# Products of constants in six pauses of TensorE, in a two-block transformer kernel

## The chip, the core and the metric

One Trainium2 chip, of which the kernel uses one core. The metric is the device time of one execution in microseconds (us), the median of several runs. Five engines work side by side, each through its own queue in order: TensorE (PE, matrix products), VectorE (DVE), ScalarE (ACT), GpSimd (POOL) and SyncE (SP, which issues transfers here). They wait for each other through semaphores. TensorE's clock has two levels, 1.2 and 2.4 GHz; the profile shows which of them was granted, as a share of the higher (0.50 or 1.00, or a mean between them).

## The reference

256 tokens of width 1024, with 16 learned tokens in front, go through two blocks, all in float32:

```python
# first block: two layers
for layer in range(2):
    h = rms_norm(hs, norm_mix_pre[layer])
    mix = pool_mixer(h, ...) if layer == 0 else sliding_window_attention(h, k_blk, v_blk, ...)
    hs = hs + rms_norm(mix, norm_mix_post[layer])
    h = rms_norm(hs, norm_ffn_pre[layer])
    hs = hs + rms_norm(swiglu(h, w_gate_up[layer], w_down[layer]), norm_ffn_post[layer])
    # after layer 0: keys and values from rms_norm(hs, kv_norm)
# second block: one layer, on the last 256 tokens
z = rms_norm_2(h, norm1_g) @ w_in            # three mixers: stick-breaking attention, mLSTM, spatial gating
h = h + concatenate([ya, yb, yc]) @ w_out
h = h + hierarchical_moe(rms_norm_2(h, norm2_g), ...)   # 32 experts, two per token
gate = sigmoid(rms_norm_2(h, ple_norm_g) @ ple_gate_w)
out = rms_norm_2(h + gate * (p @ ple_proj_w), final_g)
```

## The kernel before

Activations lie with the channels on the 128 partitions, in eight chunks of 256 or 272 tokens. Every large weight is split into a high and a low part of float32r, and so is every activation; a product is then three products of parts (`mm3`, L1268: high x high, low x high, high x low). SyncE streams the weights into `ring` (three slots), ScalarE writes the high part of each piece (L710), VectorE the low part (L720), into buffers `wh`/`wl` and `third_h`/`third_l`; each piece that is done adds one to the semaphore `lo_done`. The experts' weights go into `wring` and are used whole.

TensorE's queue runs through the stages in the order in which they are written. Between two stages lies a seam: the result must be squared, summed over the channels by a product with ones (`sum_squares`, L1259, into bank 6), turned into a factor on ScalarE (L691, L692), applied and added to the residual on VectorE and GpSimd (L1779, L564), and split into high and low parts again. TensorE has little or nothing to do meanwhile. The seams here:

- *queries* (L1306): behind the first feed-forward block. The high parts of x come one chunk at a time (`xh_ready`, ScalarE L871); for each, eight products. Then the sums, the low parts (L1312), keys and values.
- *the second feed-forward block* (`ffn_pe` with l = 1, L1199): the same pattern, x from ScalarE L805, two pieces of weights, eight products per chunk; then sums and L1207 with the low parts, then the long loop of L1268.
- *norm1*: eight sums of squares, each waiting for a square of ScalarE, then the products with `w_in` (`z`, L1268), which wait for both parts of x (`x_ready`, VectorE L1794).
- *norm2*: eight sums, then the router's products (L1592, 36 columns), 16 transposes (L1598) whose results ScalarE and VectorE split into `h2h` and `h2l`, and 32 products of the projection (L1609), whose banks ScalarE empties one after the other.
- *before the gathers*: four bfloat16 products of zeros open banks 0 to 3 (L1712), once `h2h`, `h2l` are complete; then the gathers of tokens for the first experts (L1623, L1624), which wait for VectorE's selection (`psel_ready`).
- *the last gate*: behind the sixteenth round of experts, whose results are combined in L1674, VectorE adds the experts' output to the residual and forms the low parts (L2343); the products with `w_ple` (L1268) follow, and behind the first 24 of them the eight sums of the norm.

`cst` is a table of constants in SBUF (identity, masks and the like), loaded at the start. Of the eight PSUM banks, 7 holds nothing that is still needed at the seams where the change writes it, and bank 0 nothing before L1712.

Of the kernel before, what the change touches and what calls it, by code (L numbers as in the profile page):

```python
# [7 lines left out]
BF16 = mybir.dt.bfloat16  # L8
# [6 lines left out]
P = 128  # L15
# [3 lines left out]
SEQ = 256  # L19
# [121 lines left out]
def bass_two_blocks(nc, a, out):  # L141
# [4 lines left out]
    with ctx:  # L146
# [5 lines left out]
        def sem(name):  # L152
            if name not in sems:
                sems[name] = ctx.enter_context(nc.semaphore(name))
            return sems[name]
# [24 lines left out]
        cst = sb("cst", [P, NC])  # L180
# [990 lines left out]
        def onehot(i):  # L1171

            return small[:, 200 + i * NB * NE:200 + (i + 1) * NB * NE].rearrange("p (b e) -> p b e", b=NB)

        def ffn_pe(pe, mm3, sum_squares, l, n):

            gu, dn, pre, post = f"w_gu{l}", f"w_dn{l}", f"ffnpre{l}", f"ffnpost{l}"
            xa, xb = (xhT, xlT) if l == 0 else (xh, xl)
            base = FIRST_PIECE[gu]

            def piece(i, j):
                f = i * 2 + j
                pe.wait_ge(sem("lo_done"), f + (base + 1))
                pe.wait_ge(sem("up_ready"), f + (l * NF - 1))
                w = split_buffer(gu, i, j)
                for k in range(KD):
                    for g in range(2):
                        at = slice(k * 256 + g * P, k * 256 + g * P + P)
                        ins = mm3(ps[:, 2 * j + g, 0:n], [x[:, at] for x in w], (xa[:, k, 0:n], xb[:, k, 0:n]),
                                  k == 0, k == KD - 1)  # L1190
                ins.then_inc(sem("gu_psum"), 1)

            def with_high(k):

                pe.wait_ge(sem("xh_ready"), 2 * l * KD + k + 1)
                for j in range(2):
                    for part, w in enumerate(split_buffer(gu, 0, j)):
                        for g in range(2):
                            pe.matmul(ps[:, 2 * j + g, 0:n], w[:, k * 256 + g * P:k * 256 + g * P + P], xa[:, k, 0:n],  # L1199
                                      start=(k == 0 and part == 0), stop=False)  # L1200

            def with_low(j):
                w = split_buffer(gu, 0, j)[0]
                for k in range(KD):
                    pe.wait_ge(sem("x_ready"), 2 * l * KD + k + 1)
                    for g in range(2):
                        ins = pe.matmul(ps[:, 2 * j + g, 0:n], w[:, k * 256 + g * P:k * 256 + g * P + P], xb[:, k, 0:n],  # L1207
                                        start=False, stop=(k == KD - 1))
                ins.then_inc(sem("gu_psum"), 1)

            pe.wait_ge(sem("lo_done"), base + 2)
            for k in range(KD):
                with_high(k)
            for c in range(KD):
                sum_squares(pre, c, n)
            with_low(0)
            with_low(1)
            piece(1, 0)
            piece(1, 1)
            with pe.Fori(2, NF // 2) as i:  # L1220
                for j in range(2):
                    piece(i, j)
            base = FIRST_PIECE[dn]
            for c in range(KD):
                if c >= 2:
                    pe.wait_ge(sem("sq_ready"), SQ0[post] + c - 1)
                for j in range(2):
                    pe.wait_ge(sem("lo_done"), base + 2 * c + j + 1)
                    w = split_buffer(dn, c, j)
                    for k in range(NF // 2):  # L1230
                        at = slice(k * P, (k + 1) * P)
                        f = j * (NF // 2) + k
                        if c == 0:
                            pe.wait_ge(sem("act_split"), l * NF + f + 1)
                        ins = mm3(ps[:, 4 + c % 2, 0:n], [x[:, at] for x in w],
                                  (acth[:, f, 0:n], actl[:, f, 0:n]), f == 0, f == NF - 1)
                    ins.then_inc(sem("dn_psum"), 1)
                if c:
                    sum_squares(post, c - 1, n)
            sum_squares(post, KD - 1, n)  # L1240
# [3 lines left out]
        def _(pe):  # L1244
# [54 lines left out]
                return [x[:, at] for x in split_buffer("w_q", c // 4, c // 2 % 2)]  # L1299

            pe.wait_ge(sem("lo_done"), FIRST_PIECE["w_q"] + 2)
            for k in range(KD):
                pe.wait_ge(sem("xh_ready"), KD + k + 1)
                for c in range(4):
                    for part, w in enumerate(q_weights(c, k)):
                        mm(ps[:, c, 0:SEQ], w, xh[:, k, 0:SEQ], start=(k == 0 and part == 0), stop=False)  # L1306
# [117 lines left out]
            ffn_pe(pe, mm3, sum_squares, 1, SEQ)  # L1424


            for c in range(KD):
                sum_squares("norm1", c, SEQ)
            def sgu_mix():

                pe.wait_ge(sem("sgu_v"), 1)
                pe.wait_ge(sem("sgw_masked"), 1)
                for g in range(SG):
                    ins = mm(ps[:, 7, g * P:(g + 1) * P].rearrange("p (b c) -> p b c", b=NB), sgw[:, g, :],
                             vc[:, :, g * SG_D:(g + 1) * SG_D], start=True, stop=True)
                ins.then_inc(sem("sgu_psum"), 1)
# [149 lines left out]

            for c in range(KD):
                sum_squares("norm2", c, SEQ)
            for b in range(NB):
                for k in range(KD):  # L1590
                    pe.wait_ge(sem("xn_ready"), KD + k + 1)
                    ins = mm(ps[:, 0, b * 36:(b + 1) * 36], mix[:, k, b * P:(b + 1) * P], rw[:, k, :],  # L1592
                             start=(k == 0), stop=(k == KD - 1))
# [86 lines left out]
            def extra(b):  # L1680
# [24 lines left out]
                with pe.Else():  # L1705
                    pe.sem_inc(sem("over_pe"), len(OVER["pe"]) * (ROUNDS - 1))

            pe.wait_ge(sem("h2h_ready"), 4)
            pe.wait_ge(sem("h2l_ready"), 4)
            pe.wait_ge(sem("diag_ready"), 1)  # L1710
# [44 lines left out]
            combine((yh, yl), places[(TEAMS - 1) % 2][:, :], True)  # L1755


            for c in range(KD):
                piece = FIRST_PIECE["w_ple"] + c // 2
                pe.wait_ge(sem("lo_done"), piece + 1)  # L1760
                if c >= 4:
                    pe.wait_ge(sem("ple_scaled"), c - 3)
                for k in range(KD):
                    pe.wait_ge(sem("x_ready"), 4 * KD + k + 1)
                    at = slice(k * 256 + c % 2 * P, k * 256 + c % 2 * P + P)
                    ins = mm3(ps[:, c % 4, 0:SEQ], [x[:, at] for x in split_buffer("w_ple", c // 4, c // 2 % 2)],
                              (xh[:, k, 0:SEQ], xl[:, k, 0:SEQ]), k == 0, k == KD - 1)
                ins.then_inc(sem("ple_psum"), 1)
                if c == 0:
                    for q in range(KD):  # L1770
                        sum_squares("ple", q, SEQ)
# [737 lines left out]
```

## Time and profile before

| | us |
|---|---|
| three timed runs | 1070.78, 1072.61, 1072.77 (median 1072.61) |
| the profiled execution | 1068.52 |
| its span, first to last instruction | 1066.8 |
| TensorE busy in it | 974.7 (91%) |
| VectorE, ScalarE, GpSimd busy | 540.2, 416.1, 155.6 |
| mean granted clock of TensorE | 0.954 |

The span leaves out some 1.7 us of start and end. Times inside the profile are counted from the span's start. The chain of waits that ended last is TensorE for 85% of the span. A matmul's busy time includes its way through the array, so products in a row overlap: what one costs is the distance between starts, or the length of a run divided by its count.

### The profile page before, as it was taken

The page shows a single profiled execution, that of the slowest core. Times are in us where ns is not written, and L with a number is a line of the kernel's source. Part 1 is how long each engine was busy: PE and PEld are TensorE (multiplying, and loading weights), DVE is VectorE, ACT ScalarE, POOL GpSimd, SP SyncE. Part 2 cuts the span into 40 slices and gives each one's busy share as a digit, 9 for nine tenths or more (in the row PEclk, how much of TensorE's full clock was granted, in tenths as well). Part 3 has the DMA queues.
Part 4 walks back from the last instruction along what each step waited for, and adds up shares of the span by engine and source line. Part 5 has one row for each costly group of instructions (what it writes and reads, how often), then busy time and mean ns, then how long its engine had stood idle before and what let it go on. Part 6 is the DMA issues. An engine that isn't in the chain of part 4 may idle for free.

```text
span 1066.8 us, 16807 instructions
## 1 busy us (share of the span) xinstructions
PE 974.7 (91%) x6776; PEld 819.1 (77%) x6777; DVE 540.2 (51%) x986; ACT 416.1 (39%) x697; POOL 155.6 (15%) x216
## 2 busy tenths in 40 slices
PE   3799999998989999999969999879699999999876
PEld 2599999998869899999959999578454555545365
DVE  5655454438783655554463548574523333433254
ACT  4543333347575534434454556633211111111153
POOL 5432323011001433331120000000100000000000
PEclk8899999999989999999998999788899999999988
DMA  7435453568522254534543412049079999999601
GB/s 290 157 106 202 167 172 134 189 185 205 141 80 89 93 213 158 188 131 163 214 164 127 159 52 82 1 168 396 3 283 417 420 420 420 419 420 419 260 1 40
DMA packets 36797, 211.99 MB, mean 199 GB/s; under 512 B 2528, under 2 KB 16112, under 8 KB 17520
## 3 DMA queue, kind: packets, MB, share of 16 engines
q1 hardware_dynamic: 36720, 210.91, 52.4%
q8 instruction: 55, 0.90, 0.3%
q14 instruction: 22, 0.18, 0.1%
HBM read 209.83 MB, written 1.07 MB: 198 GB/s over the span
## 4 chain that ended last, share of the span: by engine, by line
PE 85%; DVE 7%; ACT 3%; issue 2%; POOL 2%; DMA 0%; POOLq 0%; DVEq 0%; ACTq 0%
PE ps L1268 49%; PE ps L1651 11%; PE ps L1665 5%; PE ps L1259 3%; PE ps L1674 3%; PE ps L1623 2%; PE ps L1199 2%; DVE wl L720 2%; PE ps L1624 1%; DVE mix L1779 1%; PE ps L1306 1%; PE ps L1372 1%; PE ps L1207 1%; PE ps L1609 1%; PE ps L1592 1%
## 5 line engine op out<-in xcount | busy, mean ns | idle before, releaser
L720 DVE TENSOR_TENSOR wl<-ring,wh 128x2048 fp32r<-128x2048 f32 (+3 forms) x106 | 210.3, 1987 | 193.9 <-ACT wh L710 193.9
L710 ACT ACTIVATE wh<-ring 128x2048 fp32r<-128x2048 f32 (+3 forms) x106 | 176.1, 1665 | 267.2 <-PE ps L1268 265.2
L1268 PE MATMUL ps<-xh,wh 128*128 128x256 f32 (+3 forms) x632 | 180.5, 286 | 6.4 <-DVE xl L2343 6.4
L1268 PE MATMUL ps<-xh,wl 128*128 128x256 f32 (+3 forms) x632 | 179.0, 283 | 0.0
L1268 PE MATMUL ps<-xl,wh 128*128 128x256 f32 (+3 forms) x632 | 178.8, 283 | 0.0
L1268 PEld LDWEIGHTS ps<-xh,wh 128*128 128x128 f32 (+3 forms) x632 | 117.6, 186 | 7.8 <-issue 7.5
L1268 PEld LDWEIGHTS ps<-xh,wl 128*128 128x128 f32 (+3 forms) x632 | 117.6, 186 | 0.1
L1268 PEld LDWEIGHTS ps<-xl,wh 128*128 128x128 f32 (+3 forms) x632 | 117.5, 186 | 0.0
L1268 PE MATMUL ps<-acth,wh 128*128 128x272 f32 (+1 forms) x352 | 101.1, 287 | 0.0
L1268 PE MATMUL ps<-actl,wh 128*128 128x272 f32 (+1 forms) x352 | 100.0, 284 | 0.0
L1268 PE MATMUL ps<-acth,wl 128*128 128x272 f32 (+1 forms) x352 | 100.0, 284 | 0.0
L1268 PE MATMUL ps<-xhT,wl 128*128 128x272 f32 x320 | 92.6, 289 | 0.0
L1268 PE MATMUL ps<-xlT,wh 128*128 128x272 f32 x320 | 92.2, 288 | 0.0
L1268 PE MATMUL ps<-xhT,wh 128*128 128x272 f32 x320 | 91.3, 285 | 0.0
L575 POOL TENSOR_TENSOR sq<-sq 128x256 f32<-128x256 f32 (+1 forms) x15 | 19.1, 1274 | 436.0 <-ACT sq L685 436.0
L2327 DVE TENSOR_TENSOR yl<-ps,yh 128x512 fp32r<-128x512 f32 x32 | 20.6, 686 | 91.3 <-ACT yh L1137 91.3
L1268 PEld LDWEIGHTS ps<-acth,wh 128*128 128x128 f32 x352 | 66.5, 189 | 0.2
L1268 PEld LDWEIGHTS ps<-acth,wl 128*128 128x128 f32 x352 | 66.1, 188 | 0.2
L1268 PEld LDWEIGHTS ps<-actl,wh 128*128 128x128 f32 x352 | 66.2, 188 | 0.0
L1651 PE MATMUL ps<-wring,xb_even 128*64 128x512 f32 x256 | 60.0, 607 | 4.1 <-issue 4.0
L1268 PEld LDWEIGHTS ps<-xhT,wh 128*128 128x128 f32 x320 | 60.4, 189 | 0.0
L1268 PEld LDWEIGHTS ps<-xlT,wh 128*128 128x128 f32 x320 | 60.1, 188 | 0.0
(402 smaller groups left out, 1859.5 us busy)
## 6 DMA issues: line engine op xcount, KB each, us to landing
wring<-in_w_eg SPq DMA_DIRECT2D x32, 2048.0 KB, 14.3
ring<-in_w_gu SPq DMA_DIRECT2D x22, 2048.0 KB, 8.2
wring<-in_w_ed SPq DMA_DIRECT2D x16, 2048.0 KB, 12.9
ring<-in_w_dn SPq DMA_DIRECT2D x16, 1408.0 KB, 6.1
ring<-in_w_z SPq DMA_DIRECT2D x7, 2048.0 KB, 7.7
ring<-in_w_out SPq DMA_DIRECT2D x4, 1152.0 KB, 5.2
ring<-in_w_q SPq DMA_DIRECT2D x8, 512.0 KB, 6.2
ring<-in_w_o SPq DMA_DIRECT2D x8, 512.0 KB, 16.0
```

Source lines behind the costliest of these rows:

```text
L575: pool.tensor_tensor(even, even, odd, ALU.add).then_inc(sem("sq_paired"), 1)
L710: ins = act.activation(to, src, ACT.Copy)
L720: ins = dve.tensor_tensor(to, src, h.bitcast(F32), ALU.subtract)
L1199: pe.matmul(ps[:, 2 * j + g, 0:n], w[:, k * 256 + g * P:k * 256 + g * P + P], xa[:, k, 0:n], start=(k == 0 and part == 0), stop=False)
L1207: ins = pe.matmul(ps[:, 2 * j + g, 0:n], w[:, k * 256 + g * P:k * 256 + g * P + P], xb[:, k, 0:n], start=False, stop=(k == KD - 1))
L1259: mm(ps[:, 6, 0:n], ones[0:rows, :], square_at(name, c + 1 - chunks)[0:rows, 0:n], start=(c < chunks), stop=(c == last))\
L1268: ins = mm(o, p, q, start=first and n == 0, stop=last and n == 2)
L1623: mm(out, h2h[:, k, at], select[:, k, :], start=(k == 0), stop=False)
L1651: ins = mm(ps[rows, 4, :], x[:, k, rows], chunk(b, c)[:, j, i * 512:(i + 1) * 512], start=(k == 0), stop=(k == KD - 1))
L1665: ins = mm(ps[rows, 6 + i, :], heT[:, k, rows], chunk(b, GU_CHUNKS)[:, j, k * D + i * 512:k * D + (i + 1) * 512], start=(k == 0), stop=(k ...
L1674: ins = mm(ps[:, c // 2, c % 2 * SEQ:(c % 2 + 1) * SEQ], y[:, c * P:(c + 1) * P], weights, start=False, stop=last and y is parts[-1], skip ...
L2327: dve.tensor_tensor(yl[:, i * 512:(i + 1) * 512], ps[:, 6 + i, :], yh[:, i * 512:(i + 1) * 512].bitcast(F32), ALU.subtract).then_inc(sem(" ...
```

## The change

A new function, `stay_busy`, issues n products of 128 columns of constants (as bfloat16) with 512 columns of constants, each into the same bank with start and stop set, and without semaphore. It is called at seven places in TensorE's queue, at six seams: 8 at the queries, 8 in the second feed-forward block, 17 ahead of and 15 behind the sums of norm1, 4 behind the sums of norm2, 11 ahead of L1712, 24 ahead of the last gate; 87 in all. No other line changes.

```diff
+        def stay_busy(pe, bank, n):
+            weights, moving = cst[:, 0:P // 2].bitcast(BF16), cst[:, 0:SEQ].bitcast(BF16)
+            for _ in range(n):
+                pe.matmul(ps[:, bank, :], weights, moving, start=True, stop=True)
...
             pe.wait_ge(sem("lo_done"), base + 2)
+            if l:
+                stay_busy(pe, 7, 8)
             for k in range(KD):
                 with_high(k)
...
             pe.wait_ge(sem("lo_done"), FIRST_PIECE["w_q"] + 2)
+            stay_busy(pe, 7, 8)
...
             ffn_pe(pe, mm3, sum_squares, 1, SEQ)
+            stay_busy(pe, 7, 17)
             for c in range(KD):
                 sum_squares("norm1", c, SEQ)
+            stay_busy(pe, 7, 15)
...
                 sum_squares("norm2", c, SEQ)
+            stay_busy(pe, 7, 4)
...
+            stay_busy(pe, 0, 11)
             pe.wait_ge(sem("h2h_ready"), 4)
...
             combine((yh, yl), places[(TEAMS - 1) % 2][:, :], True)
+            stay_busy(pe, 7, 24)
             for c in range(KD):
                 piece = FIRST_PIECE["w_ple"] + c // 2
```

In the rows below, `ps` is PSUM, `cst` the constants, and what stands in brackets are the semaphores for which a product waits. Lines of the changed kernel are some 6 to 13 higher. TensorE at the queries' seam, before:

```order
L1268 MATMUL ps<-actl,wh 128x272
L1259 MATMUL ps<-sq,ones 128x272 [waits sq_ready] x2
L1306 MATMUL ps<-xh,third_h 128x256 [waits xh_ready,lo_done]
L1306 MATMUL ps<-xh,third_l 128x256
L1306 MATMUL ps<-xh,third_h 128x256
L1306 MATMUL ps<-xh,third_l 128x256
```

and now:

```order
L1276 MATMUL ps<-actl,wh 128x272
L1267 MATMUL ps<-sq,ones 128x272 [waits sq_ready] x2
L1179 MATMUL ps<-cst 128x512 [waits lo_done]
L1179 MATMUL ps<-cst 128x512 x7
L1315 MATMUL ps<-xh,third_h 128x256 [waits xh_ready]
L1315 MATMUL ps<-xh,third_l 128x256
L1315 MATMUL ps<-xh,third_h 128x256
```

Eight products of constants stand between the last sum of the block before and the first product with x; the first of them has taken over the wait for the split weights. TensorE at norm1, before:

```order
L1268 MATMUL ps<-actl,wh 128x256
L1259 MATMUL ps<-sq,ones 128x256 [waits sq_ready] x2
L1259 MATMUL ps<-sq,ones 128x256 [waits sq_ready,r_ready]
L1259 MATMUL ps<-sq,ones 128x256 [waits sq_ready] x7
L1268 MATMUL ps<-third_h,xh 128x256 [waits x_ready,lo_done]
L1268 MATMUL ps<-third_l,xh 128x256
L1268 MATMUL ps<-third_h,xl 128x256
```

and now:

```order
L1276 MATMUL ps<-actl,wh 128x256
L1267 MATMUL ps<-sq,ones 128x256 [waits sq_ready] x2
L1179 MATMUL ps<-cst 128x512 x17
L1267 MATMUL ps<-sq,ones 128x256 [waits sq_ready,r_ready]
L1267 MATMUL ps<-sq,ones 128x256 [waits sq_ready] x7
L1179 MATMUL ps<-cst 128x512 x15
L1276 MATMUL ps<-third_h,xh 128x256 [waits x_ready,lo_done]
L1276 MATMUL ps<-third_l,xh 128x256
L1276 MATMUL ps<-third_h,xl 128x256
```

The sums keep their waits, and a batch stands on either side of them. TensorE ahead of the gathers, before:

```order
L1615 MATMUL ps<-small,cst 128x32
L1616 MATMUL ps<-small,ones 128x32
L1617 MATMUL ps<-small,ones 128x32
L1712 MATMUL ps<-work 128x512 [waits diag_ready,h2l_ready,h2h_ready]
L1712 MATMUL ps<-work 128x512 x3
L1623 MATMUL ps<-psel,h2h 128x256 [waits psel_ready]
```

and now:

```order
L1627 MATMUL ps<-small,cst 128x32
L1628 MATMUL ps<-small,ones 128x32
L1629 MATMUL ps<-small,ones 128x32
L1179 MATMUL ps<-cst 128x512 x11
L1725 MATMUL ps<-work 128x512 [waits diag_ready,h2l_ready,h2h_ready]
L1725 MATMUL ps<-work 128x512 x3
L1635 MATMUL ps<-psel,h2h 128x256 [waits psel_ready]
```

The 11 follow the last small products of the routing directly and wait for nothing; the waits of the products that open the banks come behind them.

## Rows read from the trace of the kernel before

**Rows 1.** The page: TensorE's granted clock in 40 equal slices, in tenths.

```profile
PEclk8899999999989999999998999788899999999988
```

**Rows 2.** Stretches: length, busy PE, PEld, DVE, ACT, POOL, clock, DMA share, GB/s.

```profile
249.42:252.00 2.58, 0.00 (x0) 0.03 (x1) 1.63 (x4) 1.48 (x4) 0.20 (x1) 1.00 1.06 356
...
252.10:255.40 3.30, 3.30 (x16) 3.30 (x17) 3.23 (x7) 2.48 (x8) 1.71 (x3) 0.50 1.11 368
...
347.90:350.40 2.50, 0.00 (x0) 0.01 (x1) 1.57 (x4) 1.43 (x4) 0.19 (x1) 1.00 0.96 406
...
544.40:549.20 4.80, 0.00 (x0) 0.00 (x0) 3.83 (x8) 4.77 (x6) 1.76 (x2) 0.98 0.02 5
...
555.56:559.20 3.64, 0.00 (x1) 0.00 (x0) 3.64 (x8) 3.02 (x8) 0.00 (x0) 1.00 0.49 131
...
560.20:566.00 5.80, 5.80 (x27) 5.80 (x28) 4.40 (x8) 3.36 (x3) 0.00 (x0) 0.50 0.49 209
...
736.80:746.90 10.10, 10.10 (x44) 9.83 (x45) 5.20 (x24) 2.48 (x5) 0.00 (x0) 0.50 0.98 406
...
757.30:763.90 6.60, 4.79 (x18) 3.70 (x20) 5.27 (x22) 0.60 (x1) 2.72 (x5) 0.50 0.01 1
...
1023.05:1026.70 3.65, 3.65 (x17) 3.65 (x18) 3.11 (x7) 1.71 (x5) 1.05 (x1) 0.50 0.02 4
```

**Rows 3.** Chain that ended last: start us, length us, engine and line.

```profile
252.00 9.35 PE ps L1306 x64
...
350.42 9.42 PE ps L1199 x64
...
550.35 0.83 DVE hs L564
...
553.78 2.73 DVE wl L720
...
742.07 3.46 PE ps L1598 x16
...
745.53 7.71 PE ps L1609 x32
...
1031.52 19.95 PE ps L1268 x168
```

**Rows 4.** TensorE in order of time, router and gathers: start, length, idle before.

```profile
735.15 3.72 PE L1592 MATMUL ps<-rw,mix 128*128 128x36 f32 x17 [1.44 <-DVE mix L1779]
...
757.67 0.63 PE L1712 MATMUL ps<-work 128*128 128x512 bf16 x1 [3.41 <-issue]
...
757.67 1.49 PE L1712 MATMUL ps<-work 128*128 128x512 bf16 x3 [3.41 <-issue]
...
760.60 0.58 PE L1623 MATMUL ps<-psel,h2h 128*128 128x256 f32 x1 [1.44 <-DVE psel L1936]
```

**Rows 5.** ScalarE and GpSimd in order of time, three seams.

```profile
252.79 0.51 ACT L871 ACTIVATE xh<-hs,vec 128x256 fp32r<-128x256 f32 x1 [0.61 <-POOL hs L564]
...
351.15 0.51 ACT L805 ACTIVATE xh<-hs,vec 128x256 fp32r<-128x256 f32 x1 [0.56 <-POOL hs L564]
...
551.66 2.70 POOL L564 TENSOR_TENSOR hs<-hs,mix 128x256 f32<-128x256 f32 x1 [0.76 <-DVE mix L1779]
```

**Rows 6.** The last gate in order of time: TensorE, VectorE, ScalarE.

```profile
1023.05 0.55 PE L1268 MATMUL ps<-xh,wh 128*128 128x256 f32 x1 [6.42 <-DVE xl L2343]
...
1027.69 1.03 PE L1259 MATMUL ps<-sq,ones 128*128 128x256 f32 x4
...
1022.43 3.73 DVE L2343 SCALAR_TENSOR_TENSOR xl<-hs,vec,xh 128x256 fp32r<-128x256 f32 x8
...
1028.32 1.33 ACT L685 ACTIVATE sq<-hs 128x256 f32<-128x256 f32 x4 [3.56 <-PE ps L1259]
```

**Rows 7.** Stretches that the change doesn't touch, columns as in rows 2.

```profile
303.30:310.00 6.70, 6.70 (x39) 5.08 (x38) 6.56 (x27) 3.36 (x13) 0.00 (x0) 0.50 0.25 51
...
774.20:777.60 3.40, 3.40 (x10) 1.43 (x11) 0.00 (x0) 0.00 (x0) 0.00 (x0) 0.52 0.00 0
```

## What the change should do to the time

> **What bounds the kernel now.** I read the page first: TensorE is busy for 91% of the span and makes up 85% of the chain that ended last, and in ten of the 40 slices its granted clock is below nine tenths [rows 1]. So TensorE sets the time, and part of its work is done at the lower of its two clock levels (1.2 GHz, granted 0.50) instead of the higher (2.4 GHz, granted 1.00). Then I read stretches at the seams between stages [rows 2]: each time the engine has nothing to do (busy 0.00) and the row behind it, where it works again, has clock 0.50. At 249.42 it stops for 2.58 us, and the next 3.30 us of work run at 0.50; from 555.56 it does nothing for 3.64 us, and the 5.80 us of work from 560.20 run at 0.50. The rows that end in a bracket [rows 4, 6] give three more such pauses, 1.44, 3.41 and 6.42 us, with 0.50 behind them at 736.80, 757.30 and 1023.05 [rows 2]. Behind the 2.50 us at 347.90 the same loop as at 252.00 is as long as there, 9.42 against 9.35 us [rows 3]. The chain of waits [rows 3] shows that the work behind the pauses is itself on the path to the end, in long unbroken pieces of TensorE.
>
> What a product costs at either level: 168 split products of 256 columns took 19.95 us at 1.00, so 0.119 us each [rows 3]; 17 of them fill 3.65 us at 0.50, so 0.214 us each [rows 2]. A stretch of low clock of length t in which the engine works without waiting costs 1 - 0.119/0.214 = 0.44 t.
>
> **The change part by part.** Nothing is removed or moved. 87 products of 512 columns are added (8, 8, 17, 15, 4, 11, 24), none with a semaphore of its own, all into a bank that its next user starts anew. The nearest row for such a product is L1712, bfloat16, 512 columns, at 0.50: three in 1.49 us, of which one alone is 0.63, so (1.49 - 0.63)/2 = 0.43 us each [rows 4]. At 1.00 I take half, 0.22 us (by the ratio of the 256-column products it would be 0.24). So the batches last 1.8, 1.8, 3.7, 3.3, 0.9, 2.4 and 5.3 us if the clock holds. What hides them are the pauses: 2.58, 2.50, 4.80, 4.6 (555.56 to 560.20), 1.44, 3.4 and 6.4 us [rows 2, 4, 6]. Each is shorter than its pause, so the batches themselves cost nothing; if the clock were low throughout, the first two would last 3.4 us and overrun by 0.9 us each. Two of them now take over the wait for the split weights (lo_done), which was met before the pause began.
>
> *The queries' seam* (8 products, then L1306, 64 products from 252.00, 9.35 us [rows 3]). At 1.00 throughout, eight products per chunk of x need 0.95 us. The second chunk comes only at 252.79 + 0.51 = 253.30 [rows 5]; with the 0.14 us from there to TensorE and 7 x 0.95 the loop ends at 260.1 and not at 261.35. Gain 1.25 us; bounds 0 and 0.44 x 3.4 = 1.5. The sums, L1312 and ScalarE's next split (it waits for L1312) follow TensorE, so it is passed on.
>
> *The second feed-forward block* (8, then L1199, 64 products in 9.42 us from 350.42 [rows 3]). Likewise: second chunk at 351.66 [rows 5], end at 351.80 + 6.65 = 358.45 and not 359.84. Gain 1.4 us; bounds 0 and 1.5. L1207 then waits for nothing: x's low parts and the pair sums are done by about 360.
>
> *norm1* (17 ahead of the eight sums, 15 behind). The sums are set by VectorE and GpSimd, not by TensorE: the last add of the stream, on GpSimd, takes 2.70 us from 551.66, and normalising can't start before a split on VectorE ends at 553.78 + 2.73 = 556.51 [rows 3, 5]. So the 17 gain nothing. The 15 stand ahead of L1268, whose first 5.8 us run at 0.50 [rows 2]: worth 0.44 x 5.8 = 2.6 us. Off this goes a new hole: the last add but one ends at 550.35 + 0.83 = 551.18 [rows 3]; with its square and its sum, some 0.4 us each, TensorE is then through at about 552.1, and does nothing until the last add is done at 554.36, about as long as at 249.42, where the clock fell. If it falls here, some 8 of the 15 run at 0.43, as long as the low stretch at 252.10, and 7 at 0.22: 5.0 us, from the end of the last sum at 555.56 until 560.5 instead of 560.20. I take 2.3 us; bounds 0.8 (all 15 at 0.43, 1.8 us over) and 2.6.
>
> *norm2* (4). The clock falls into the router's products (L1592) and stays at 0.50 for 10.10 us although the engine is counted busy all that time [rows 2], with 36-column products and then transposes [rows 3, 4]. Four products move that fall later, they don't stop it. At best everything to 746.9 runs high: the last 16 of L1592 and the 16 transposes, 0.216 us each [rows 3], save 0.094 each or 3.0 us, and the first 1.4 us of L1609 0.7, together 3.7 us; at worst 0. I take 0.7, near the low end, for 0.9 us of work against 10 us of low clock. It is passed on: ScalarE empties L1609's banks one by one and VectorE's routing waits for that.
>
> *Before the gathers* (11). The four products of L1712 aren't on the path: the first gather waits for the selection made by VectorE until 760.60 [rows 4]. After them TensorE has some 2 us of nothing again, so I expect the 16 gather products still mostly at 0.50. Bounds 0 and 16 x 0.094 = 1.5; I take 0.3.
>
> *The last gate* (24, ahead of L1268 at 1023.05, after 6.42 us idle [rows 6]). Its first products run at 0.50 [rows 2] and the sums behind the first 24 start at 1027.69. With the clock high they keep pace with x's low parts, eight in 3.73 us from 1022.43, so until 1026.16 + 0.14 + 3 x 0.119 = 1026.7. Gain 1.0 us, passed on since ScalarE's last four squares wait for those sums [rows 6]; bounds 0 and 1.7.
>
> Sum: 1.25 + 1.4 + 2.3 + 0.7 + 0.3 + 1.0 = 7.0 us. Against the profiled execution, 1068.52 us with a span of 1066.8, that is 1061.5; the three timed runs lie 2 to 4 us above it, at a median of 1072.61, and the forecast goes by that: **1065.6 us**.
>
> The rule of the Trainium skill that weighs here is in "TensorE: Matmul & The Clock Gate", Part 4 (PE-mode transpose): the high clock doesn't engage for transposes. The trace agrees as far as it goes, with 0.50 through all 16 of L1598 [rows 2, 3]. By it alone norm2's batch would gain nothing and the sum would be 6.3.
>
> **The rivals.** *Everything holds.* norm2 and the gathers reach their upper bounds: 3.0 + 1.2 us more, 1061.4. Against it speaks that both have a thin stretch right behind the batch.
>
> *The clock falls elsewhere.* The idle time before a fall isn't one number: below 2.6 us at 249.42, above 4.6 at 544.40 (0.98 over 4.80 us) [rows 2]. So where a fall comes depends on something beside the work, and low stretches that the change doesn't touch, 6.70 us at 303.30 and 3.40 at 774.20 [rows 7], can come out longer after the shift. One more low stretch like that at 774.20 (0.44 x 3.4 = 1.5 us), the two seams with the shortest pauses falling in only half of the runs even before (half of 1.25 + 1.4, 1.3 us), and nothing from norm2 (0.7) take 3.5 us off the gain: 1069.1. The same page says (Part 1, What's actually happening) that the gate's window runs free of the kernel, so the switch falls differently from run to run; these rows agree, and by it no single run gives the sum above.
>
> *The products don't count.* No row shows bfloat16 products of constants raising the clock; the four of L1712 came and went at 0.50. If the gate ignores them, every fall comes where it did, the batches of the first seams are over by then, and only the 24 lose something: by 1020 about 15 are done, 9 more at 0.43 end at 1023.9, 0.8 us late. 1073.4, no change.
>
> *Slower: the batches run at the low level.* If the clock is down when the 15 and the 24 start and they don't bring it back, they take 6.45 and 10.3 us, 1.8 and 3.9 us past their pauses, with L1268 behind them still at 0.50: 1078.3. It decides from the point where a batch at 0.43 is longer than its pause. Against it: the clock came back under ordinary work each time.
>
> **How the numbers follow.** Forecast 0.50, everything holds 0.13, falls elsewhere 0.20, don't count 0.10, slower 0.07. A measurement of this kernel tells 0.2% (2.1 us) from no change. Faster by more: 0.50 + 0.13 + 0.17 of the third = 0.80; within: the rest of the third and the fourth, 0.13; slower 0.07. The range runs from 1061 (the upper case) to 1071 (beyond the third case), leaving out most of the last two.
>
> **What would show it.** Right: granted clock 1.00 in L1306, in L1199 and in the first z products; L1306 some 8.1 us long, L1199 8.0 us; L1268 behind norm1 starting within 0.4 us of 4.7 us after the last sum; mean clock above 0.954. Wrong in size: the fall merely moved into the sums or the gathers. Wrong altogether: L1306's first products still 0.214 us apart behind eight constant products, or a first product of a stage that waits for a batch and not for x.

## The result, and the profile after

The changed kernel took **1057.61 us** (median of 8 runs, 1055.99 to 1065.58), the kernel before, beside it, 1070.26 us (8 runs, 1065.18 to 1072.77): a ratio of 0.9888, 95% interval 0.9865 to 0.9911. So it is faster by 12.0 us, with 9.5 to 14.4 in the interval. The forecast had the direction right and the size wrong: 7.0 us of gain, 1065.6 us, and a range whose lower end was 1061. The profiled execution lasted 1058.62 us. The ratios here and below leave out runs over 1.5% above the fastest of their kernel: one of six of the kernel with only the 15 behind norm1's sums, and five of twelve of that with 143 narrow products.

The page after, its span and granted clock:

```profile
span 1056.9 us, 16974 instructions
...
PEclk8799999999999999999999999789799999999998
```

Beside [rows 1] the eights of slices 12, 22, 28 and 39 are gone (slice 12 is the stretch around 303 us, where nothing was added; slice 22 holds z's start, slice 28 the router), and six slices are below nine tenths, where there were ten. The mean granted clock is 0.967 instead of 0.954.

TensorE after, in order of time, at norm1 and at the last gate (start, length, what, idle before and releaser):

```profile
543.75 3.62 PE L1179 MATMUL ps<-cst 128*128 128x512 bf16 x16
548.62 3.26 PE L1267 MATMUL ps<-sq,ones 128*128 128x256 f32 x14 [1.25 <-ACT sq L685]
554.21 0.70 PE L1267 MATMUL ps<-sq,ones 128*128 128x256 f32 x2 [2.33 <-ACT sq L685]
554.74 3.40 PE L1179 MATMUL ps<-cst 128*128 128x512 bf16 x15
559.55 0.36 PE L1276 MATMUL ps<-third_h,xh 128*128 128x256 f32 x1 [1.41 <-DVE xl L1808]
...
1006.54 5.13 PE L1179 MATMUL ps<-cst 128*128 128x512 bf16 x23
1014.33 0.36 PE L1276 MATMUL ps<-xh,wh 128*128 128x256 f32 x1 [2.67 <-DVE xl L2357]
```

One record each of the 17 and of the 24 is missing from the trace. Fifteen of the products take 3.40 us, 0.23 each, where the forecast for the high clock was 0.22. Behind the 15 and behind the 24 the stage's first product waits for VectorE's xl, not for the batch. Stretches after (columns as in rows 2):

```profile
253.96:262.33 8.37, 8.14 (x65) 7.93 (x66) 8.27 (x17) 7.14 (x16) 3.75 (x4) 1.00 1.08 284
...
559.55:566.00 6.45, 6.45 (x54) 6.45 (x55) 4.41 (x8) 3.82 (x4) 0.16 (x2) 1.00 0.46 198
...
736.90:740.30 3.40, 3.40 (x19) 3.40 (x19) 2.79 (x15) 1.79 (x3) 0.00 (x0) 0.51 1.02 424
740.42:747.20 6.78, 6.78 (x33) 5.96 (x32) 2.63 (x13) 3.38 (x9) 0.00 (x0) 1.00 0.47 195
...
754.03:764.27 10.24, 8.58 (x34) 7.74 (x35) 4.37 (x14) 1.20 (x2) 2.69 (x4) 0.50 0.00 1
...
1014.40:1017.80 3.40, 3.13 (x23) 2.93 (x24) 3.05 (x7) 1.64 (x5) 1.06 (x1) 1.00 0.00 0
```

At the queries, at z (norm1) and at the last gate the clock is 1.00, where [rows 2] had 0.50. At the router only 3.4 us are left of the 10.1 at 0.50. Around the gathers it is worse than before: 10.24 us at 0.50, the four products of L1734 behind them included, and before 6.6.

Where the two executions drift apart, by the starts of the same products (before, after, and the distance of after from before):

| product | before | after | distance |
|---|---|---|---|
| first of the queries (L1306, now L1315) | 252.00 | 253.96 | +1.96 |
| first of z (L1268, now L1276) | 560.20 | 559.55 | -0.65 |
| gating products amid the z stage (L1434, L1445) | 598.00 | 594.71 | -3.29 |
| router (L1592, L1604) | 735.15 | 732.05 | -3.10 |
| first gather (L1623, L1635) | 760.60 | 754.74 | -5.86 |
| first expert product (L1651, L1663) | 771.33 | 767.72 | -3.61 |
| first down product (L1665, L1677) | 785.78 | 779.39 | -6.39 |
| last team but one, combining (L1674, L1686) | 990.62 | 982.65 | -7.97 |
| last combining | 1013.05 | 1004.32 | -8.73 |
| first sum of the last gate (L1259, L1267) | 1027.69 | 1017.97 | -9.72 |

The execution starts with a loss of 2 us that no added product explains (none has run by then): the clock was low for 6.7 us in the first feed-forward block. From there to the first expert product the changed kernel gains 5.6 us, and 1.0 at the last gate, together 6.6; of this some 0.5 us lies between the queries and the second feed-forward block, where nothing was added. But 5.1 us come from another place where nothing was added, between the first expert product and the last combining. What changed there shows in TensorE's order of time, first team of experts, before:

```profile
771.33 1.04 PE L1651 MATMUL ps<-wring,xb_even 128*64 128x512 f32 x2 [2.23 <-issue]
774.12 4.43 PE L1651 MATMUL ps<-wring,xb_even 128*64 128x512 f32 x11 [1.75 <-issue]
```

and after:

```profile
767.72 4.87 PE L1663 MATMUL ps<-wring,xb_even 128*64 128x512 f32 x13 [2.20 <-issue]
```

Before, the engine stopped for 1.75 us after two of the products, with nothing to wait for ("issue"), and the clock was low behind that hole [rows 7, second row]. From the first expert product to the first down product it took 14.45 us before, and 11.67 after. The experts' waits as a whole, 764 to 1012 us (waited for: us in total, times, longest), before:

```profile
PE ps L1651 <- issue: 5.2, 4, 2.2
```

and after:

```profile
PE ps L1663 <- issue: 2.2, 1, 2.2
```

### The profile page after: what moved, and what is told of

It is laid out like the page before. It is cut to its first block, busy times and chain, and to the rows that moved or that the text cites. A ratio compares the mean times of both kernels' runs of the same rounds, so it can differ in the third digit from the quotient of the medians.

```text
span 1056.9 us, 16974 instructions
## 1 busy us (share of the span) xinstructions
PE 982.0 (93%) x6858; PEld 813.5 (77%) x6864; DVE 540.0 (51%) x986; ACT 416.2 (39%) x697; POOL 155.7 (15%) x216
## 4 chain that ended last, share of the span: by engine, by line
PE 85%; DVE 8%; ACT 3%; POOL 2%; issue 2%; DMA 0%; POOLq 0%; DVEq 0%; ACTq 0%
PE ps L1276 49%; PE ps L1663 11%; PE ps L1677 5%; PE ps L1267 3%; PE ps L1686 3%; PE ps L1635 2%; PE ps L1205 2%; PE ps L1636 2%; DVE wl L720 2%; DVE mix L1793 1%; PE ps L1213 1%; PE ps L1621 1%; PE ps L1315 1%; DVE third_l L720 1%; PE ps L1296 1%
## 5 line engine op out<-in xcount | busy, mean ns | idle before, releaser
L1276 PE MATMUL ps<-xh,wh 128*128 128x256 f32 (+3 forms) x632 | 180.0, 285 | 2.9 <-DVE xl L2357 2.9
L1276 PE MATMUL ps<-xh,wl 128*128 128x256 f32 (+3 forms) x632 | 178.4, 282 | 0.0
L1276 PE MATMUL ps<-xl,wh 128*128 128x256 f32 (+3 forms) x632 | 178.2, 282 | 0.0
L1276 PEld LDWEIGHTS ps<-xh,wh 128*128 128x128 f32 (+3 forms) x632 | 116.8, 185 | 4.7 <-issue 4.0
L1276 PEld LDWEIGHTS ps<-xh,wl 128*128 128x128 f32 (+3 forms) x632 | 116.8, 185 | 0.1
L1276 PEld LDWEIGHTS ps<-xl,wh 128*128 128x128 f32 (+3 forms) x632 | 116.7, 185 | 0.0
L1276 PE MATMUL ps<-acth,wh 128*128 128x272 f32 (+1 forms) x352 | 101.1, 287 | 0.0
L1276 PE MATMUL ps<-actl,wh 128*128 128x272 f32 (+1 forms) x352 | 100.0, 284 | 0.0
L1276 PE MATMUL ps<-acth,wl 128*128 128x272 f32 (+1 forms) x352 | 100.0, 284 | 0.0
L1276 PE MATMUL ps<-xhT,wl 128*128 128x272 f32 x320 | 92.6, 289 | 0.0
L1276 PE MATMUL ps<-xlT,wh 128*128 128x272 f32 x320 | 92.2, 288 | 0.0
L1276 PE MATMUL ps<-xhT,wh 128*128 128x272 f32 x320 | 91.3, 285 | 0.0
L1276 PEld LDWEIGHTS ps<-acth,wh 128*128 128x128 f32 x352 | 66.5, 189 | 0.2
L1276 PEld LDWEIGHTS ps<-acth,wl 128*128 128x128 f32 x352 | 66.1, 188 | 0.2
L1276 PEld LDWEIGHTS ps<-actl,wh 128*128 128x128 f32 x352 | 66.2, 188 | 0.0
L1663 PE MATMUL ps<-wring,xb_even 128*64 128x512 f32 x256 | 58.5, 607 | 2.2 <-issue 2.2
L1276 PEld LDWEIGHTS ps<-xhT,wh 128*128 128x128 f32 x320 | 60.4, 189 | 0.0
L1276 PEld LDWEIGHTS ps<-xlT,wh 128*128 128x128 f32 x320 | 60.1, 188 | 0.0
```

What stands on the lines that cost most here:

```text
L1276: ins = mm(o, p, q, start=first and n == 0, stop=last and n == 2)
L1663: ins = mm(ps[rows, 4, :], x[:, k, rows], chunk(b, c)[:, j, i * 512:(i + 1) * 512], start=(k == 0), stop=(k == KD - 1))
```

## The experiments

Two theories stood at the start. **Clock**: the gain is what the products do to TensorE's clock. **Position**: part of it comes from products, each with its weight load, standing ahead of the experts' code (63 of the 87 do), whatever they compute. Each group of kernels has its own 15 to 22 runs of the kernel before beside it, and ratios are to those. "Narrow" means 16 columns instead of 512; such a product does next to no work.

### All 87 narrow

```diff
-            weights, moving = cst[:, 0:P // 2].bitcast(BF16), cst[:, 0:SEQ].bitcast(BF16)
+            weights, moving = cst[:, 0:P // 2].bitcast(BF16), cst[:, 0:8].bitcast(BF16)
-                pe.matmul(ps[:, bank, :], weights, moving, start=True, stop=True)
+                pe.matmul(ps[:, bank, 0:16], weights, moving, start=True, stop=True)
```

> All 87 added products stay where they are, but each has 16 columns instead of 512. Theory one (the work of the products keeps the clock up): a 16-column product is next to no work, so every fall of the clock comes back and the time is that of the kernel before, ratio 0.998 to 1.002, mean granted clock near 0.954. Theory two (a good part of the gain comes from the position of the code, because 174 more instructions shift what is fetched when, and holes inside groups of the experts' products close): the ratio stays at 0.995 to 0.997 and the holes of 0.5 to 1.8 us between products of one group, of which the kernel before has five (4.2 us together over the usual spacing) and the changed one two, are as few as in the changed kernel.

Measured: 1063.72 us (11 runs), ratio 0.9949 (0.9933 to 0.9964), with the changed kernel unaltered beside it at 1058.75 us (6 runs), 0.9919 (0.9889 to 0.9949).

> The changed kernel unaltered, timed and profiled once more. Theory one: ratio 0.987 to 0.991 again; in its profile the products behind the four seams of the attention, feed-forward, norm1 and last gate run at 1.00 again, while the low stretches elsewhere (start, mixers, gathers) lie at other places than in the first profile. Theory two: the few holes in the experts' stage are there again as few and as short, since they come from the code's position; if they are many this time, they are chance.

The clock stayed as before: mean 0.952, and z's start at the low level (stretch in this kernel, columns as in rows 2):

```profile
561.60:568.30 6.70, 5.93 (x28) 5.96 (x29) 5.17 (x10) 4.21 (x5) 0.00 (x0) 0.50 0.55 235
```

Yet 5.5 us of the gain are there (3.9 to 7.2 by the interval). From the first expert product to the first down product it takes 10.03 us instead of 14.45, and from there to the first sum of the last gate 239.4 instead of 241.9. So about half of the gain is there without the work that was to hold the clock up. (Some of it is clock all the same: the low stretch at 774.20 [rows 7] stood behind the hole of 1.75 us, and it is gone with that.)

### Without the 4 and the 11

```diff
-            stay_busy(pe, 7, 4)
...
-            stay_busy(pe, 0, 11)
```

> The change without the 4 products behind norm2's sums and the 11 ahead of the gathers; 8, 8, 17, 15 and 24 stay. By the two profiles the 4 gave 2.8 us (norm2's sums to the end of the projection) and the 11 nothing. If the 4 are worth what the first profile says, this kernel is 2 to 3 us slower than the whole change, ratio 0.990 to 0.992, and L1604 to L1621 take 19.6 to 20.5 us again instead of 16.9; if that was the luck of one execution, the ratio is that of the whole change, 0.987 to 0.990.

Measured: 1058.96 us (6 runs), 0.9908 (0.9885 to 0.9932), the same as the changed kernel beside it. The router is again at the low level throughout (stretch in this kernel):

```profile
735.00:745.00 10.00, 10.00 (x45) 9.67 (x45) 5.14 (x24) 2.49 (x5) 0.00 (x0) 0.50 0.99 410
```

In these times both batches together are worth nothing that can be told, and a gain of the forecast 1.0 us can't be told from it either: the intervals reach some 2.5 and 3.2 us to either side. (The traces say more, see the table in the next part.) The 2.8 us which the first profile shows at the router stand against 1.7 us lost at the gathers. The unaltered changed kernel, run again beside this one, had all its gathers at the high clock, where its first profile has 10.24 us at 0.50:

```profile
753.00:773.00 20.00, 13.69 (x74) 8.02 (x76) 12.28 (x44) 4.05 (x7) 5.05 (x8) 1.00 0.01 1
```

### Only the 15 behind norm1's sums

```diff
-                stay_busy(pe, 7, 8)
...
-            stay_busy(pe, 7, 8)
...
-            stay_busy(pe, 7, 17)
...
-            stay_busy(pe, 7, 4)
...
-            stay_busy(pe, 0, 11)
...
-            stay_busy(pe, 7, 24)
```

> Only the 15 products behind norm1's sums. Theory one: the products of z start at the high clock, and the time from there to the first product of the gating (L1445) is 35.2 us instead of 37.8; ratio 0.997 to 0.999 (2.0 to 2.6 us), with nothing gained elsewhere beyond chance. If the 17 ahead of the sums are needed for that (the sums then run low and the clock is still down when the 15 start), the 15 take up to 6.4 us, z starts up to 1.8 us late and the gain is 0.8 us or less. Theory two expects less than half of the holes closed here, since only 30 instructions are added.

Measured: **1082.32 us** (6 runs, 1076.83 to 1093.44), 1.0126 (1.009 to 1.0163): slower than before, though z's start was at clock 1.00 as meant. The experts' waits, same stretch and columns as above:

```profile
PE ps L1663 <- issue: 13.1, 7, 3.4
```

The loss lies wholly in the experts' stage. Neither the clock theory nor the forecast has a place for that. The next kernels were to tell whether the fifteen did it by their work or by their number.

### Fifteen narrow ones, and forty-eight

```diff
             for c in range(KD):
                 sum_squares("norm1", c, SEQ)
+            stay_busy(pe, 7, -15)
```

A negative number here and below stands for so many narrow products. All other calls are left out; in the second kernel 48 stand in place of 15.

> The kernel before with one thing added: fifteen products of 16 columns behind norm1's last sum; they hold TensorE for next to nothing and leave its clock alone. Theory position (what counts in the experts' stage is how many instructions of TensorE stand ahead of it): holes between the experts' products come back every second or third round as in the kernel with only the fifteen full products, some 15 to 20 us in all, time 1078 to 1088, expected 1083. Theory work (the fifteen full products themselves did the harm, by their 3 us at z's start or by the clock): time as before, 1069 to 1071, with the few holes of the kernel before.

Measured: **1090.69 us** (6 runs, 1083.71 to 1095.57), 1.0191 (1.0149 to 1.0232). Fifteen products that do next to nothing make the kernel 20 us slower.

> The kernel before with forty-eight products of 16 columns behind norm1's last sum. Theory position: as many instructions stand ahead of the experts' stage as in the kernel without the four and the eleven, which has no hole there, so the first round's hole of 1.75 us at 772 us and the four at 895 to 997 us go: 1063 to 1065. Theory work: 1069 to 1071, holes unchanged. If the place of the added instructions counts and not only their number, holes lie elsewhere, and the time is between the two or above.

Measured: 1063.73 us (10 runs), 0.9953 (0.9937 to 0.997), as with all 87 narrow. Waits in the experts' stage with 15, and then with 48:

```profile
PE ps L1663 <- issue: 20.0, 7, 3.8
```

```profile
PE ps L1663 <- issue: 2.2, 1, 2.2
```

Position decides, in both directions. One of the holes with 15, TensorE in order of time:

```profile
829.39 3.65 PE L1677 MATMUL ps<-wring,work 128*64 128x512 f32 x16
832.87 1.02 PE L1663 MATMUL ps<-wring,xb_even 128*64 128x512 f32 x2
836.58 1.51 PE L1663 MATMUL ps<-wring,xb_even 128*64 128x512 f32 x6 [2.68 <-issue]
```

The list of queues for the 0.2 us from 834.00 in that kernel (packets, MB, share of 16 engines):

```profile
q1 hardware_dynamic: 8, 0.07, 77.4%
q8 instruction: 1, 0.02, 34.0%
```

The page has 55 packets of instructions, 0.90 MB, some 16 KB each. One of them is under way from 834.1, inside the hole, and 2.5 us after its start TensorE goes on. The same holds for all 21 holes of over half a microsecond behind which an experts' product follows, in this kernel, in the kernel before, with the fifteen wide ones and with the 143 below (the 2.2 us ahead of the stage's first product set aside): TensorE goes on 2.3 to 2.9 us after a packet's start. So "issue" means here, as far as the traces can tell, that the engine has no code to run. In 20 of the 21 the hole comes after at most three products behind `extra(b)`, which jumps over the code for teams with too many tokens; in one, in the kernel before, after twelve.

A packet at this place doesn't make a hole by itself. In the kernel before one starts at 834.4, 1.0 us after the first product of the same team, and the products go on:

```profile
833.46 7.03 PE L1651 MATMUL ps<-wring,xb_even 128*64 128x512 f32 x31
```

With 48, packets start at 827.2 and 835.6, and there is no hole either. That the fifteen make it the block which is needed at once is inferred, not seen: the trace doesn't say which code a packet brings.

### 143 narrow ones

128 more than fifteen, at the same place (the diff is as above, with 143).

> The kernel before with 143 products of 16 columns behind norm1's last sum, that is 15 and 128 more. TensorE's instructions come in packets of 16 KB (q8 in the page's list of queues: 55 packets, 0.90 MB), and in the trace three arrive in two rounds of the experts' stage. Theory blocks (what decides is where a block's edge lies in the code of the experts' stage; 128 products with their weight loads are 256 instructions, an estimate of one block): as with 15, long holes in every second round, 1085 to 1095 plus some 3 us for the products themselves. Theory number (the more stands ahead, the better, or it is the distance in time): time near the kernel with 48, 1064 to 1068, few holes.

Measured: 12 runs from 1067.89 to 1095.13 us, median 1083.52, less than the 1088 to 1098 that were expected. Even the seven lowest give 1.0039 (1.0003 to 1.0075), above the 0.9953 of 48. The profiled execution is one of the longest, 1091.94 us. Waits in its experts' stage:

```profile
PE ps L1663 <- issue: 17.2, 8, 3.5
```

The holes are back, in this execution nearly of the size that fifteen brought, and so more instructions ahead aren't better as such. That speaks for the blocks, where what counts is where an edge between blocks of code falls. A period of 128 products isn't shown: five of the twelve runs lie below 1075 us, where all six with fifteen took 1083 or more, and a scan over the numbers in between wasn't made.

### Without the branch

TensorE's code for overfull teams is left out; these inputs never use it, a kernel for any input needs it. Once with the fifteen narrow ones, once with nothing added.

```diff
             def extra(b):
-                count = busiest(pe, b)
-                with pe.If(count > FEW):
...
-                with pe.Else():
-                    pe.sem_inc(sem("over_pe"), len(OVER["pe"]) * (ROUNDS - 1))
+                pe.sem_inc(sem("over_pe"), len(OVER["pe"]) * (ROUNDS - 1))
```

> The kernel with fifteen products of 16 columns (1090.7 us), and TensorE's program of the experts' stage without the code for overfull teams: no branch over it, no code there; it is never run with these inputs, but a kernel for any input needs it. Theory jump (the holes, all at the first products behind that branch, come from a jump to code that isn't there yet): all holes go, time 1060 to 1066, the 20 us of holes gone. Theory queue (code fetched late whatever the order, because the weights fill the queues): holes stay wherever a block ends, more than 5 us in all, time above 1070.

Measured: 1063.39 us (11 runs), 0.9938 (0.9916 to 0.996). The same fifteen products that cost 20 us with the branch cost nothing without it.

> The kernel before without that branch and its code on TensorE, and nothing added. Theory jump: no hole in the experts' stage, so the 1.75 us and the low clock behind it in the first round and the four holes at 895 to 997 us go, and it is within 2 us of the kernel with fifteen products and no branch: 1060 to 1066. Theory queue: as before, 1069 to 1071, or holes of another size.

Measured: 1062.83 us (6 runs), 0.9928 (0.99 to 0.9956). Neither kernel has a wait for "issue" in the experts' stage, not even the 2.2 us ahead of its first product, and the page of both has 13 packets of instructions fewer:

```profile
q8 instruction: 42, 0.69, 0.3%
```

With the branch gone position no longer matters at the two numbers tried, and the kernel before gains by it what 48 or 87 narrow products bring it. That ties the second half of the gain to this branch. The edit takes out three things at once: reading the team's count, the jump, and the code behind it; which of them is needed for the holes wasn't tried. A fixed cost of reading the count is no rival for the rest, since it can't depend on whether 15 or 48 products stand ahead.

### norm1 alone and the other seams alone, at the same position

The changed kernel with all 87 products in their places, but only some of them wide: first norm1's 17 and 15, then the 8, the 8 and the 24.

```diff
-            stay_busy(pe, 7, 4)
+            stay_busy(pe, 7, -4)
...
-            stay_busy(pe, 0, 11)
+            stay_busy(pe, 0, -11)
```

(and so on for the others; what is wide is named above)

> The changed kernel with only norm1's 17 and 15 products at full width, the other 55 at 16 columns: every instruction stands where it does in the changed kernel. Against the kernel with all 87 at 16 columns (0.9949 of before): the prediction's term for norm1 says 2.3 us less, the profile's shifts 2.6, so 1064.1 - 2.3 to 2.6 = some 1061.7 (0.9926). If the clock's stretches fall elsewhere instead: 1064. Holes in the experts' stage: 0 to 2 as in the changed kernel, not the twenty us of the kernel with the fifteen alone.

Measured: 1060.24 us (6 runs), 0.9924 (0.99 to 0.9948). That is 0.0025 or 2.7 us under all narrow; expected were 2.3 to 2.6. The intervals, 1.7 and 2.6 us to either side, are as wide as that, so the agreement is partly luck; the trace bears it out (next part).

> The changed kernel with only the 8, 8 and 24 products of the queries' seam, the second FFN block and the last gate at full width, the others at 16 columns, so that all instructions keep their places. The prediction's terms: 1.25 + 1.4 + 1.0 = 3.65 us below the kernel with all 87 at 16 columns, so 1064.1 - 3.65 = some 1060.5 (0.9915). If those products only move the low stretches elsewhere: 1064.

Measured: 1061.63 us (6 runs), 0.9936 (0.9911 to 0.9961). That is 1.4 us under all narrow, and 3.65 were expected; the intervals reach 1.7 and 2.7 us to either side, so this says "less than forecast" only weakly. The trace shows where it can come from: behind the 24 wide products the clock was low all the same (stretch right behind the first product of the last gate):

```profile
1017.30:1020.60 3.30, 3.30 (x17) 3.30 (x17) 2.91 (x7) 1.50 (x4) 1.04 (x1) 0.50 0.00 0
```

### A version with one more batch

The changed kernel without the 4 and the 11, and with the 8 in the first feed-forward block too.

```diff
-            if l:
-                stay_busy(pe, 7, 8)
+            stay_busy(pe, 7, 8)
...
-            stay_busy(pe, 7, 4)
...
-            stay_busy(pe, 0, 11)
```

> The changed kernel without the 4 and the 11, whose absence cost nothing, and with the eight products in the first FFN block too (before its first products, in a pause of 2.6 us behind which the clock was low for 3.4 to 6.8 us in most kernels run here). 56 products stand ahead of the experts' stage, between 48 and 63, which both had next to no holes. Theory clock: 1 to 3 us below the changed kernel, so 1055 to 1058. If the low stretch only moves, or the eight hold up the first products: 1058 to 1060.

Measured: 1056.21 us (6 runs, 1054.97 to 1059.01), 0.9874 (0.9847 to 0.9902), the lowest of all. In the first block the clock now holds (stretch in this kernel, where the changed kernel has 6.7 us at 0.50 from 44.1):

```profile
40.00:54.00 14.00, 12.54 (x81) 10.29 (x81) 9.82 (x17) 9.47 (x21) 6.11 (x7) 1.00 0.77 301
```

Its interval overlaps that of the changed kernel, so that it beats it is likely, not shown. Nor does the trace settle it: the queries' first product starts at 252.36 us, and the other traces, none of which has this batch, have it anywhere from 251.62 to 254.51.

## Why the prediction was wrong

**What bounds the kernel** was read rightly as far as it went: TensorE, partly at its low clock, and each batch fitted into its pause. What the views held beside it and the prediction didn't use was the "issue" among TensorE's waits. The hole of 1.75 us that ended at 774.12 and those of 0.68 and 0.54 us that ended at 984.86 and 996.90 were in the trace of before, and the low stretch at 774.20 stood in [rows 7] as one that the change doesn't touch. The change did touch it.

**The failed step** is the first sentence of the part on the change: "Nothing is removed or moved", with 87 products priced by their duration alone. All code behind them was moved: 63 of the products stand ahead of the experts' stage, which with their weight loads begins 126 instructions later. Measured with the products made narrow, this is worth 5.5 us (3.9 to 7.2). It could as well have been a loss: at fifteen it is 20 us the other way, more than all clock terms together. No rival had this mechanism, and none of the five cases came below 1061.4.

**The clock's terms.** The sum was 7.0 us. Wide against narrow products at the same position gives 5.0 us in one comparison (1063.72 against 1058.75) and 0.9949 - 0.9888 = 0.0061, or 6.5 us, with the runs of the first result. So the sum was near, if a little high. The 14 traces show the seams one by one, each as the distance between two starts (us; "wide" means that this seam's own products were there at full width):

| stretch | wide | without or narrow |
|---|---|---|
| queries, first to last product of L1315 | 8.08 to 8.09 (5 traces) | 9.06 to 9.56 (9) |
| second feed-forward block, L1205 likewise | 8.02 to 8.09 (5) | 9.14 to 10.28 (8), 7.93 (1) |
| norm1, first of z to first gating product | 35.15 to 35.53 (6) | 36.65 to 37.93 (8) |
| router's first to first expert product | 35.67, 33.39 (2) | 35.95 to 36.42 (10) |
| last combining to first sum of the last gate | 13.63 to 13.65 (4), 14.44 (1) | 14.59 to 15.27 (9) |

(The two kernels without the branch aren't in the fourth row, since their 2.2 us ahead of the first expert product is gone.)

- *Queries, second block:* L1315 ends 8.37 us after its first product (forecast 8.1), L1205 8.30 us (350.88 to 359.18; forecast 8.0). Gains 1.0 and 1.1 us for 1.25 and 1.4, against the one trace of before.
- *norm1:* 2.3 forecast; 2.64 by the profile (the distance grows from -0.65 to -3.29), 2.7 by the experiment. The feared fall of the clock between the sums didn't come, and the 15 took 3.40 us instead of 5.0. Whether the 17 have a part in it wasn't tried at the same position; in the kernel with the fifteen alone, without them, the clock was low for 6.8 us from 548.3 on and z's start still at 1.00.
- *norm2:* 0.7 forecast with an upper bound of 3.7; the profile after shows 2.8. *Gathers:* 0.3 forecast; the profile shows 1.7 us lost between the first gather and L1734. Over the whole stretch the two executions of the changed kernel are 0.5 and 2.8 us shorter than before, while the ten traces without wide batches lie within 0.3 us of before. Their low stretches are the same each time, 10.2 us at the router and 6.8 ahead of the gathers; with both batches they were 3.4 and 10.2 us in one execution, 6.8 and none in the other. So the sum, forecast at 1.0, is of the right order in the traces, and the times without both batches can't confirm it. (The second execution of the changed kernel spent its 2.8 us elsewhere: from the first gating product to the router it took 138.56 us, the kernel without both batches 134.92.)
- *Last gate:* 1.0 us forecast; the distance grows from -8.73 at the last combining to -9.72 at the sums, so 1.0.
- The clock also fell where it hadn't in the trace of before (first block, +2 us), ahead of every added product, so that isn't the change's doing. The rival "the clock falls elsewhere" had low stretches that come and go; its time, 1069.1, was on the wrong side.

**The rule on transposes.** By the Trainium skill ("TensorE: Matmul & The Clock Gate", Part 4: PE-mode transpose) the high clock doesn't engage for transposes, which would have made norm2's batch worth nothing. In the execution after, the 16 transposes were at 0.51 and the 32 products right behind them at 1.00. But in two other traces, the second of the changed kernel and that without the branch and with nothing added, the clock came back amid the transposes: twelve start 0.21 us apart, and the last four follow 0.11 us apart. The end of them in the changed kernel's second trace:

```profile
745.30:745.90 0.60, 0.60 (x7) 0.60 (x6) 0.50 (x3) 0.49 (x2) 0.00 (x0) 1.00 0.92 382
```

So transposes did run at the high clock here, twice in 14 traces. What keeps the clock down through all 16 in the others stays open.

**The base.** The forecast stood on a median of three runs, 1072.61; eight more give 1070.26, and the kernel before spreads from 1065.0 to 1075.6 over its runs beside the experiments. From 1070.26 the same sum would have given 1063.3, so 2.4 of the 8.0 us by which the time was missed are the base, and the rest is the gain.

## What to carry to other kernels

Added instructions have two prices: their time, and what they do to the position of all code behind them. Where the trace shows "issue" holes behind a jump over code that isn't run, measure a change also with its instructions made idle: only the difference to that belongs to its idea. And such holes are worth removing for themselves, by fewer jumps over long code or by padding: forty-eight idle products brought this kernel 5 us. How many is a matter of this very code: fifteen cost it 20 us.

## What the runs showed of the hardware

- Behind a jump over a long piece of code TensorE stood for 0.5 to 3.8 us at a time, in all 17.8 us in the trace with fifteen narrow products and none in the two traces without the branch. The profile's queue q8 carries packets of some 16 KB, and TensorE went on 2.3 to 2.9 us after one had started, in all 21 such holes.
- A hole costs twice. The clock may fall behind it, as at 774.20 [rows 7] and here, with fifteen narrow products, behind the one that ended at 903.51:

```profile
904.00:907.40 3.40, 3.40 (x11) 1.37 (x9) 2.18 (x9) 0.00 (x0) 0.00 (x0) 0.50 1.00 378
```

- And the weights' transfers, 417 GB/s on average over 790 to 990 us in the kernel before, wait for buffers that TensorE then frees late: 380 GB/s with the fifteen narrow products. So a hole there isn't made up for.
- bfloat16 products of constants do hold the clock up: at the queries, in the second feed-forward block, at z and at the last gate the stage behind them ran at 1.00 in the changed kernel, and with narrow ones z's start was at 0.50. How long the clock stays is not theirs alone: one of five traces with the 24 has 3.3 us at 0.50 right behind them, and ahead of the gathers the same eleven were followed by 10.24 us at 0.50 in one execution and by 20 us at 1.00 in another.
